# Attention of a hybrid decoder step: a head's P is turned one head later, and the sample values take P as weights

## The reference

```
s = einsum(q, keys) * 64**-0.5       # 16 heads of 64, 4 KV heads
s = where(selected, s, -inf)         # at most 256 keys per query, causal
p = softmax(s);  o = einsum(p, values)
merged = sigmoid(g_att) * o + sigmoid(g_ssm) * ssd
```

## Time and profile before

| | |
|---|---|
| median of 3 runs | 2578.71 us (2577.3 to 2583.53) |
| the profiled execution | 2578.58 us, its span 2576.8 us |
| PE busy | 2281.0 us, 89% |
| DVE busy | 1473.3 us, 57% |
| ACT, POOL busy | 605.2 us, 837.1 us |
| granted clock, mean | 0.93 |

### The profile page before, as it was taken

One profiled execution on the slowest core, in us unless ns is written; L12 is line 12 of the kernel. 1 busy time (PEld: TensorE's weight loads), 2 busy tenths in 40 slices (PEclk: granted clock), 3 DMA queues, 4 the chain that ended last, 5 costly groups with the idle time before them and its releaser, 6 DMA issues.

```text
span 2576.8 us, 34162 instructions
## 1 busy us (share of the span) xinstructions
PE 2281.0 (89%) x13287; PEld 2069.7 (80%) x13287; DVE 1473.3 (57%) x2413; ACT 605.2 (23%) x1005; POOL 837.1 (32%) x728
## 2 busy tenths in 40 slices
PE   7898999999999757755877879879999999999995
PEld 3893479999999756644666665679999999999995
DVE  1724345999999957766877654426432323233237
ACT  2213311010023232234655551102201000010103
POOL 0210034233333153424554331251242433424235
PEclk9997999999999978877999887669999999999997
DMA  6114322222222133225211006430210110101122
GB/s 266 62 48 141 131 82 98 90 98 82 92 88 98 49 96 80 65 57 108 50 33 25 17 1 205 164 122 33 83 66 33 48 49 33 65 33 51 47 83 82
DMA packets 110372, 203.22 MB, mean 79 GB/s; under 512 B 10405, under 2 KB 78005, under 8 KB 98741
## 3 DMA queue, kind: packets, MB, share of 16 engines
q1 hardware_dynamic: 94610, 163.90, 19.8%
q10 hardware_dynamic: 15670, 38.19, 3.9%
HBM read 161.06 MB, written 41.13 MB: 78 GB/s over the span
## 4 chain that ended last, share of the span: by engine, by line
PE 41%; DVE 5%; issue 3%; ACT 2%; DMA 2%; POOL 2%; SPq 1%; DVEq 0%; POOLq 0%; ACTq 0%
PE pj L1878 30%; PE px L1325 5%; PE pj L1559 2%; DVE Pr L1449 2%; PE pj L1314 2%; ACT PT L1378 1%; DMA raw<-in_w_out 1%; PE pj L1518 1%; PE pj L1302 1%; DMA kv_w<-in_cache_kv 1%; PE pj L1301 0%; SPq L1477 0%; POOL wlo L1835 0%; DVE M L1412 0%; ACT Pr L1353 0%
## 5 line engine op out<-in xcount | busy, mean ns | idle before, releaser
L240 PE MATMUL pj<-act_hi,whi 128*128 128x344 f32 x1344 | 430.1, 320 | 3.5 <-POOL wlo L223 2.3
L240 PE MATMUL pj<-act_hi,wlo 128*128 128x344 f32 x1344 | 429.2, 319 | 0.0
L240 PE MATMUL pj<-act_lo,whi 128*128 128x344 f32 x1344 | 428.9, 319 | 0.0
L1878 PE MATMUL pj<-ahi,whi 128*128 128x344 f32 x816 | 263.2, 323 | 12.5 <-DVE alo L2034 10.5
L215 POOL CAST whi<-raw 128x512 fp32r<-128x512 f32 (+2 forms) x100 | 66.8, 693 | 622.4 <-PE pj L240 397.3
L1878 PE MATMUL pj<-ahi,wlo 128*128 128x344 f32 x816 | 261.4, 320 | 0.0
L1878 PE MATMUL pj<-alo,whi 128*128 128x344 f32 x816 | 261.0, 320 | 0.0
L240 PEld LDWEIGHTS pj<-act_hi,whi 128*128 128x128 f32 x1344 | 252.6, 188 | 3.8 <-issue 2.6
L240 PEld LDWEIGHTS pj<-act_hi,wlo 128*128 128x128 f32 x1344 | 252.5, 188 | 0.0
L240 PEld LDWEIGHTS pj<-act_lo,whi 128*128 128x128 f32 x1344 | 252.2, 188 | 0.0
L1878 PE MATMUL pj<-u_lo,d_hi 128*128 128x344 f32 x720 | 230.6, 320 | 0.0
(11 more groups left out here) (373 smaller groups left out, 4753.1 us busy)
## 6 DMA issues: line engine op xcount, KB each, us to landing
raw<-in_w_in SPq DMA_DIRECT2D x29, 1024.0 KB, 4.9
raw<-in_w_ada SPq DMA_DIRECT2D x24, 1024.0 KB, 4.9
raw<-in_w_up SPq DMA_DIRECT2D x16, 1024.0 KB, 4.8
raw<-in_w_down SPq DMA_DIRECT2D x16, 1024.0 KB, 4.8
scr_g<-O ACTq DMA_DIRECT2D x16, 516.0 KB, 2.7
scr_c<-E ACTq DMA_DIRECT2D x16, 516.0 KB, 2.7
xb<-scr_c SPq DMA_DIRECT2D x8, 1024.0 KB, 6.7
qt<-scr_q SPq DMA_DIRECT2D x32, 256.0 KB, 5.4
```

The source lines that it names most:

```text
L240: ins = pe.matmul(pj[:, hs, n, 0:W3], w[:, hs, k], a[:, k, c], start=(k == 0 and m == 0), stop=(k == kt - 1 and m == 2))
L1878: ins = pe.matmul(out, a[:, k], b[:, k, c], start=(k == 0 and m == 0), stop=(k == kt - 1 and m == 2))
```

## The change

In the attention PE turns head n-2 beside the score of n+2, and the values products, DVE's gate and its add follow one head later. In the sample stage P is the weights (16 columns) and V moves (256 columns), so that the result of a sample is 16 rows (heads) by 256 columns. ACT copies these rows of a pair to SBUF, and four transposes (`flip`) put them where `heads(g)` was before. The SBUF room is part of the tile `early`, into which POOL later splits weights; so POOL waits for the last flip before its second pair of blocks. In the sample turn a wait for the copy of two pairs before is dropped.

```diff
             for n in range(N_HEADS + 4):
                 if n + 2 < N_HEADS:
                     score(n + 2)
-                if 1 <= n <= N_HEADS:
-                    turn(n - 1)
-                if n >= 4 and n % 2 == 0:
-                    values(n // 2 - 2)
+                if 2 <= n <= N_HEADS + 1:
+                    turn(n - 2)
+                if n >= 5 and n % 2 == 1:
+                    values((n - 5) // 2)
...
-            for n in range(N_HEADS + 6):
-                if n >= 9 and n % 4 == 1:
+            for n in range(N_HEADS + 7):
+                if n >= 10 and n % 4 == 2:
                     gate(n // 4 - 2)
...
-                if n >= 9 and n % 4 == 1:
+                if n >= 10 and n % 4 == 2:
                     add(n // 4 - 2)
...
+        heads_out = cst[0:16, K_COS:K_COS + 512]
...
                 pe.wait_ge(SA["pn"], g + 1)
-                if g >= 2:
-                    pe.wait_ge(SA["ptc"], 2 * (g - 1))
...
                 if o == 0:
                     pe.wait_ge(SA["ptc"], 2 * g + 2)
-                for j in range(2):
-                    out = heads(g)[:, o, j]
-                    for k in range(8):
-                        pe.matmul(out, kv[b % 4][:, k, 256 + j * P:256 + j * P + P], sT[:, g % 2, k, 16 * o:16 * o + 16],
-                                  start=(k == 0), stop=False)
-                    ins = pe.matmul(out, vn[0:8, NT, j * P:j * P + P], s8[:, g % 2, 16 * o:16 * o + 16], start=False, stop=True)
-                ins.then_inc(SA["o"], 1)
+                out = pj[0:16, g % 2, 2, 256 * o:256 * o + 256]
+                for k in range(8):
+                    pe.matmul(out, sT[:, g % 2, k, 16 * o:16 * o + 16], kv[b % 4][:, k, 256:512], start=(k == 0), stop=False)
+                pe.matmul(out, s8[:, g % 2, 16 * o:16 * o + 16], vn[0:8, NT], start=False, stop=True).then_inc(SA["o"], 1)
+
+            def flip(g):
+
+                pe.wait_ge(SA["hc"], g + 1)
+                for o in range(2):
+                    for j in range(2):
+                        ins = pe.transpose(heads(g)[:, o, j], heads_out[:, 256 * o + j * P:256 * o + j * P + P], ident[0:16, 0:16])
+                ins.then_inc(SA["ft"], 1)
...
                 if g < NB // 2 - 1:
                     keys(2 * g + 2)
                     spread(2 * g + 2)
+                    if g:
+                        flip(g - 1)
                     keys(2 * g + 3)
                     masked(g + 1)
                     spread(2 * g + 3)
+                else:
+                    flip(g - 1)
                 turn(g)
                 values(2 * g)
                 values(2 * g + 1)
+            flip(NB // 2 - 1)
...
+            def own_heads(g):
+
+                act.wait_ge(SA["o"], 2 * g + 2)
+                if g:
+                    act.wait_ge(SA["ft"], g)
+                act.activation(heads_out, pj[0:16, g % 2, 2], ACT.Copy).then_inc(SA["hc"], 1)
+
             for g in range(NB // 2):
+                if g:
+                    own_heads(g - 1)
                 store_state(2 * g)
...
+            own_heads(NB // 2 - 1)
             act.wait_ge(SS["g"], 1)
...
-                dve.wait_ge(SA["o"], 2 * g + 2)
+                dve.wait_ge(SA["ft"], g + 1)
...
                 if n == 1:
+                    pool.wait_ge(SA["ft"], NB // 2)
```

More of the change, by code:

```diff
@@ L1468, in program @@
         s_mh, s_ml = sem("s_mh"), sem("s_ml")
-        SA = {n: sem("smp_" + n) for n in ("s", "nm", "p", "pn", "pt", "ptc", "o", "att")}
+        SA = {n: sem("smp_" + n) for n in ("s", "nm", "p", "pn", "pt", "ptc", "o", "hc", "ft", "att")}
         SS = {n: sem("sss_" + n) for n in ("dt", "dtc", "e", "ec", "dec", "bx", "bc", "s1", "new", "y", "g", "sq", "ss", "rt", "m")}
```

## The result

The changed kernel took 2506.35 us (median of 4 runs, 2501.5 to 2513.4) beside 2578.01 us (2576.0 to 2583.5) for the kernel before on the same chip: a ratio of 0.9721, 95% interval 0.9691 to 0.9751. Forecast were 2501.0 us and a range of 2484 to 2535. The profiled execution took 2503.6 us with a span of 2501.8, so 75.0 us of span went (71.7 by the medians), where the prediction had 77.5. The mean granted clock rose from 0.93 to 0.946.

What follows compares the result with a forecast made beforehand. No engine fills the attention or sample stage; an order of waits holds PE, with the clock at half in the old values. Attention -59.0 and samples -18.5 make -77.5 us, from 2578.6 to 2501; range 2484 to 2535.

Steps and rivals of the forecast that it cites:

- chain reduction, exponential, copy, turn: Attention: PE's turn waits for ACT's copy behind an exponential awaiting DVE's reduction; 1.91 us once in two heads, 61.7 in all.
- my first sign of being right: Attention, tiles 4 to 7: no wait for ACT's copy of the turned head remains before PE's turns.
- The rate when the stall is gone: Attention: each tile runs at its busiest engine plus something; tiles 4 to 7 at 45.6, 48.0, 53.3, 73.8 us.
- The work that the clock gives back: Attention: without gaps PE's half-clock work shrinks, 7.1 us back in tile 6, 8.7 in tile 7 and tail.
- The new wait at nothing: Attention: DVE's reduction of head n+2 waits for a turn behind that head's score; 0.93 us in tile 6, covered, cost nothing.
- one of my signs of being wrong: Attention: DVE idle behind a turn in tiles 4 to 7 would show the prediction wrong.
- Values with P as weights: Sample stage: a pair takes 10.0 us for 16.3, half clock for 4.5 us, then full; four pairs -25.2 us.
- What is given back: Sample stage: page loads +3.2, warmer keys -1.5, ACT in last pair +4.1, last heads +1.3, squares -0.4 us.
- Clock at half in the values: Rival, sample stage: values stay at half clock, 15.5 us a pair for 16.3; samples +2, total 2522 us; chance 0.13.
- DVE in the place of the stall: Rival, attention: DVE waits for turn after turn, PE keeps gaps; attention -31, total 2529 us; chance 0.15.
- Slower by a closed ring: Rival, attention: reduction and score wait on each other through the turn within one head; total 2608 us; chance 0.03.
- Half of the sample gain given back to the pages: Rival, sample stage: page loads fill the stage and give back half its gain; total 2510 us; chance 0.07.

Runs made afterwards that it cites:

- the kernel with both edits of the samples: Changed kernel with SP's state load of sample b-1 ahead of sample b's pages, and ACT's copy of the previous pair's heads behind the exponential: 2492.6 us, ratio 0.9660.

## Why the prediction was right

**The cause.** The chain reduction, exponential, copy, turn was read from six rows, and it is shown: the kernel with only the copy moved has PE's old order, none of the change, and the same tiles 4 to 7 within 1 us. The wait did not go altogether, which was my first sign of being right: 16.5 of the 61.7 us are left. To move the copy ahead in the change as well made tiles 4 to 7 only 1.4 us shorter.

**The sum.** That it came within 2 us (-75.6 for -77.5) is in part luck: the tiles gave 2.0 us more than forecast and the sample stage 3.9 less, and two wrong terms of that stage, treated below, offset each other.

**The rate when the stall is gone.** Each tile was set at its busiest engine and something more: 45.6, 48.0, 53.3, 73.8 against 44.3, 46.3, 52.0, 73.7. Over its busiest engine tile 4 needs 1.7 us more, tile 5 2.0 and tile 6 2.5; I had given 3.0, 3.8 and 4.2. The work that the clock gives back was right: PE in tile 6 was to be 49.1 us and is 49.5, in tile 7 68.3 and is 68.7.

**The new wait at nothing.** For the wait that this was said of it holds. The reductions wait for a turn in tiles 6 and 7 alone (11.4 us, 14 times), where DVE is not the busiest engine, and these tiles came out at 52.0 and 73.7 us for 53.3 and 73.8. DVE idle behind a turn in tiles 4 to 7 was one of my signs of being wrong; it was there and cost nothing, so it was a poor sign. Mis-sized is what happened in tiles 1 to 3, -1.6 where -4.0 stood. PE's waits for the scaled P fell from 15.6 to 1.9 us, but PE now waits 11.6 us there for reductions, and DVE 9.3 us for turns that it is to copy out. The prediction named this second wait and gave it no price; in tile 3 it costs 1.0 to 2.7 us.

**Values with P as weights.** 10.0 us a pair forecast, 9.9 to 10.3 measured in the four pairs (5.43 + 0.55 and 3.56 + 0.55 us the first). The split that I took, half clock and then full, holds as well: the first sample's sixteen records take 5.2 to 5.7 us, the second's 3.56. The figure is no constant: in the 44 pairs of the eleven traces with these products a pair takes 8.2 to 11.2 us, by how much of it is at half clock. The Trainium skill ("TensorE: Matmul & The Clock Gate", What's actually happening) has half clock as the default state, which activity releases. The trace agrees for the new products, 5.95 of 6.00 us busy at 0.69 and then 1.00. For the old ones it does not: 8.00 of 8.00 us busy at 0.50.

**What is given back.** The step that failed most. It priced two queues, the page loads and ACT's copy. The pages grew nearly as priced, PE's waits for them by 2.9 us where I had 3.2, though by a slip: I set 3.9 us of values per sample against SP's 5.8, and my own 10.0 us a pair make it 5.0. What I overlooked, and so put at nothing, is the third thing behind the pages on SP, the state loads. With values of 10 us a pair in place of 16.3, a state comes late, DVE's update of it comes late, and the scaling of P and the gate are queued behind that update. PE waits 4.0 us for the gate. The gap from pair 1 to 2 grew to 28.1 us where I had 23.5; in the three gaps 58.5 us stand against a forecast of 52.2, 6.3 more. With the state loads moved ahead, the waits for the gate are gone from the trace and 6.3 us of the stage came back. Not separated is why the gate was so late. In these two gaps the scaling instructions took 2.0 and 2.9 us longer than their shortest time (last section), which would cover PE's waits there, 1.1 and 3.0 us, nearly to the end; with the states ahead these instructions are short again. Against it the end of the stage is 3.4 us shorter than forecast, mostly because the squares take 1.90 us where I had taken 3.1, and the last split on DVE 0.52 us where it took 1.96 before.

**The rivals.** Clock at half in the values: false, 0.69 and then 1.00. DVE in the place of the stall: false as put, since the tiles came out 1.7 to 2.5 us above their busiest engines (tile 7 with its tail 5.0); DVE binds tile 4, but by its own work (the passes), not by waiting for turns. Slower by a closed ring: false, PE's wait for a reduction is 15.2 us in all, 22 times, and tiles 1 to 3 became no longer. Half of the sample gain given back to the pages: in kind this happened, by a quarter, and for the most part to another transfer. The two gaps with loads grew by 6.8 us (2.3 and 4.5) of the 25.2 that the values gave.

## What to carry to other kernels

When an engine waits for a copy, look first at what the copy stands behind on its own in-order engine: four lines moved there were worth as much as a new order of two engines, without the new wait. When a stretch that covered loads is cut, list every transfer queued behind those loads, and every instruction queued behind the one that consumes them; the one that comes late need not be the one that was priced. And filler work that was spread evenly belongs where its engine has slack: once the stall was gone, the passes of tile 4 made it 4.7 us longer than it had to be, but the place they are moved to must have slack as well.

## What was not expected of the hardware

Two DVE instructions of the sample stage took several times their own time where POOL worked on large tiles beside them: the scaling of 32x1025 takes 0.74 us or 2.14, the one of 32x8 behind it 0.22 us or 1.75 to 2.32. In the timeline of the changed kernel the small one begins during a split on POOL and both end together, at 1554.58 and 1554.56:

```profile
1551.67 2.89 POOL L1674 TENSOR_TENSOR alo<-M,ahi 128x1024 fp32r<-128x1024 f32 x1 [5.21 <-ACT ahi L1614]
...
1552.39 2.19 DVE L1724 TENSOR_SCALAR p_own<-cst,sS 32x8 f32<-32x8 f32 x1
```

In the kernel before the large one took 2.4 to 2.6 us in two of four pairs and the small one 0.22 in all; in the change the small one is slow in three pairs, and in the kernel with both edits of the samples neither is slow in any. That POOL is the reason was not tried; the traces only show the two side by side. It matters, since just these two stand before the gate and the turn that PE waits for.

And the clock did not follow PE's busy time alone. Through the old values it read 0.50 over 8.00 us without a gap; the new ones, which also begin at half clock, read 1.00 behind the first sample.
